# Hybrid decoder step: state-space rounds with the gelu stores issued by ScalarE, two rounds' tables loaded first, the first scan between the scaled blocks, and a table in the weight ring

## The reference, cut to what matters

```
u = h.reshape(bsz, L, S5_GROUPS, S5_GROUP)                 # 64 groups of 16 channels
bu_re, bu_im = einsum('gpc,blgc->blgp', bb, u)             # 64 complex states per group
pr, pi, sr, si = associative_scan(s5_combine, (ar, ai, bu_re, bu_im), axis=1)
y = einsum(c_re, st_re) - einsum(c_im, st_im) + d_skip * u
y = gelu(y)
pg = y @ w_glu
out = pg[..., :D] * sigmoid(pg[..., D:])
```

## Time and profile before

| what | us |
| --- | --- |
| median of 3 runs | 3763.41 |
| the profiled execution | 3765.0 |
| its span | 3763.3 |
| PE busy | 3483.8 |
| s5 phase, end of ffn0 to the first glu matmul (2571.7 to 2762.3) | 190.6 |
| PE busy in it | 99.9 |

### The profile page before, as it was taken

How to read it: one execution, slowest core, us unless ns; L and a number is a source line. 1 busy time by engine, 2 the same in 40 slices (tenths; PEclk the granted TensorE clock), 3 DMA queues, 4 the chain that set the end, 5 groups by cost and what they waited for, 6 DMA issues and landing times.

```text
span 3763.3 us, 56314 instructions
## 1 busy us (share of the span) xinstructions
PE 3483.8 (93%) x23339; PEld 3372.6 (90%) x23339; DVE 2151.3 (57%) x4475; ACT 830.3 (22%) x1753; POOL 840.4 (22%) x773
## 2 busy tenths in 40 slices
PE   6999999999999999998799999996579899999998
PEld 5989898999989898987799999995479799999997
DVE  5666768586766666775656765745622433333434
ACT  3333233323232332323001001001210200000001
POOL 2202020202020111201232322322323133333331
PEclk8999999999999999999899999998689899999999
DMA  2111111111111111110112222224821011111111
GB/s 94 47 36 47 40 42 38 53 37 47 33 50 41 47 44 44 41 34 24 36 53 82 69 77 82 64 74 145 233 55 45 28 49 49 46 45 51 46 45 63
DMA packets 106413, 214.19 MB, mean 57 GB/s; under 512 B 24240, under 2 KB 58416, under 8 KB 105136
## 3 DMA queue, kind: packets, MB, share of 16 engines
q1 hardware_dynamic: 77536, 169.20, 14.4%
q10 hardware_dynamic: 28624, 41.38, 3.4%
HBM read 169.47 MB, written 41.07 MB: 56 GB/s over the span
## 4 chain that ended last, share of the span: by engine, by line
PE 75%; DVE 19%; issue 2%; DMA 2%; ACT 1%; SPq 1%; POOL 0%; POOLq 0%; DVEq 0%; ACTq 0%
PE ps L215 23%; PE ps L585 15%; PE ps L1275 12%; PE ps L744 4%; PE ps L662 4%; PE ps L740 3%; PE ps L730 3%; PE ps L231 1%; DVE dwork L1202 1%; PE ps L637 1%; PE ps L292 1%; DVE S L1094 1%; DMA uu<-keep_u 1%; DVE n_r L1529 1%; PE ps L597 1%
## 5 line engine op out<-in xcount | busy, mean ns | idle before, releaser
L215 PE MATMUL ps<-hhi,whi 128*128 128x344 f32 x2424 | 778.8, 321 | 20.1 <-DVE hlo L1739 16.2
L215 PE MATMUL ps<-hhi,wlo 128*128 128x344 f32 x2424 | 776.1, 320 | 0.0
L215 PE MATMUL ps<-hlo,whi 128*128 128x344 f32 x2424 | 775.2, 320 | 0.0
L2004 POOL TENSOR_TENSOR wtick<-wtick 128x1 f32<-128x1 f32 x213 | 43.5, 204 | 2727.3 <-PE ps L215 828.9
L2007 POOL TENSOR_TENSOR wlo<-wraw,whi 128x1024 fp32r<-128x1024 f32 x213 | 529.9, 2488 | 17.1
L215 PEld LDWEIGHTS ps<-hhi,whi 128*128 128x128 f32 x2424 | 457.4, 189 | 22.8 <-issue 17.9
L215 PEld LDWEIGHTS ps<-hhi,wlo 128*128 128x128 f32 x2424 | 457.0, 189 | 0.0
L215 PEld LDWEIGHTS ps<-hlo,whi 128*128 128x128 f32 x2424 | 456.7, 188 | 0.1
L1364 DVE TENSOR_TENSOR ab<-ps,sg 128x344 f32<-128x344 f32 x132 | 68.2, 516 | 600.4 <-PE ps L215 583.5
L585 PE MATMUL ps<-hhi,whi 128*128 128x344 f32 x1152 | 387.1, 336 | 1.8 <-DVE dwork L952 1.8
L1275 PE MATMUL ps<-ahi,whi 128*128 128x344 f32 x1056 | 343.0, 325 | 33.5 <-DVE ab L1364 26.7
(11 more groups left out here) (345 smaller groups left out, 6226.3 us busy)
## 6 DMA issues: line engine op xcount, KB each, us to landing
wraw<-in_w SPq DMA_DIRECT2D x213, 512.0 KB, 3.5
dwork<-keep_rows SPq DMA_DIRECT2D x64, 256.0 KB, 3.2
tab<-keep_tab SPq DMA_DIRECT2D x8, 1088.0 KB, 6.5
S<-in_sin ACTq DMA_DIRECT2D x16, 512.0 KB, 3.7
out_sout<-S ACTq DMA_DIRECT2D x16, 512.0 KB, 2.7
keep_u<-hs SPq DMA_DIRECT2D x8, 580.0 KB, 3.0
uu<-keep_u SPq DMA_DIRECT2D x8, 580.0 KB, 7.8
keep_tab<-cp ACTq DMA_DIRECT2D x8, 576.0 KB, 6.5
```

Source lines behind the costliest of these rows:

```text
L215: ins = nc.tensor.matmul(out, w, r[:, kt, blk(n)], start=k == 0, stop=k == 3 * KT - 1)
```

## The change

The stores of `yg` go from SP to ACT, which issues them right after the gelu of the same round. `ee0` (scan table of the even rounds) and the inner table of the odd rounds lie in the two slots of `wraw`; the outer table of the odd rounds has its own room, and `hs` has its own; `yg` lies in the first buffer of `hs`. SP loads the tables of round 0 and the inner and outer tables of round 1 before the first block is stored; the scan table of round 1 follows the eighth block. DVE runs scan(0) after three scaled blocks and the other five after it. In SP's loop all loads of round r+2 stand before the state's store of round r, the scan table ahead of the outer one. Two fewer weight units are loaded before the phase; they follow it, behind waits for PE's inner(7) and DVE's xp(6).

```diff
-        ee0 = s_("ee0", [P, 2, PQ, NBLK])
+        ee0 = wraw[:, 1, :].rearrange("p (a q n) -> p a q n", a=2, q=PQ)
...
-        tab = [tab0, s_("tab1", [P, TABW])]
-        yg = s_("yg", [P, 2 * PQ, XC])
+        hs = s_("hs", [P, 3, STEP, UC])
+        tab1 = s_("tab1", [P, TABW - TWT])
+        inner_tab, outer_tab = [tab0[:, 0:TWT], wraw[:, 0, :]], [tab0[:, TWT:TABW], tab1[:, :]]
+        yg = hs[:, 0].rearrange("p a n -> p (a n)")[:, 0:2 * PQ * XC].rearrange("p (g n) -> p g n", n=XC)
...
-            def inputs(r):
+            def inner_table(r):
                 o = r % 2
                 if r >= 2:
                     s.after("PE", f"vv{r - 2}.1")
+                sp.dma_start(inner_tab[o], keep_tab[r, :, 0:TWT]).then_inc(inner_in[o], 16)
+
+            def load_u(r):
                 if r >= 3:
                     s.after("PE", f"y{r - 3}.1")
-                sp.dma_start(tab[o][:, 0:TWT], keep_tab[r, :, 0:TWT]).then_inc(inner_in[o], 16)
                 sp.wait_ge(u_store[r], 16)
...
-            def tables(r):
+            def outer_table(r):
+                o = r % 2
+                if r >= 2:
+                    s.after("PE", f"y{r - 2}.1")
+                sp.dma_start(outer_tab[o], keep_tab[r, :, TWT:TABW]).then_inc(outer_in[o], 16)
+
+            def scan_table(r):
                 o = r % 2
                 if r >= 2:
                     s.after("PE", f"y{r - 2}.1")
                     s.after("DVE", f"xp{r - 2}")
                     s.after("POOL", f"sto{r - 2}")
-                sp.dma_start(tab[o][:, TWT:TABW], keep_tab[r, :, TWT:TABW]).then_inc(outer_in[o], 16)
                 sp.dma_start(eel[o][:, :, :, :], keep_ee[r]).then_inc(outer_in[o], 16)
                 sp.dma_start(xp[o][:, :, :, NBLK + 1:XC], dr["s5i"][r]).then_inc(outer_in[o], 16)
...
-            tables(0)
+            inner_table(0)
+            outer_table(0)
+            sp.wait_ge(w_split, glu0 + 2)
+            inner_table(1)
+            scan_table(0)
+            outer_table(1)
             store_u(0)
-            inputs(0)
-            for kt in range(1, KT):
+            store_u(1)
+            load_u(0)
+            store_u(2)
+            load_u(1)
+            for kt in range(3, KT):
                 store_u(kt)
-            for kt in range(KT):
-                sp.wait_ge(u_store[kt], 16)
-            inputs(1)
-            tables(1)
+            scan_table(1)
             for r in range(SR):
                 if r + 2 < SR:
-                    inputs(r + 2)
-                s.after("ACT", f"ge{r}")
-                for j in range(STEP):
-                    sp.dma_start(keep_y[r].rearrange("(g c) j n -> j c g n", c=G16)[j], yg[G16 * j:G16 * (j + 1), :, :]).then_inc(y_store, 16)
-                if r + 2 < SR:
-                    tables(r + 2)
+                    inner_table(r + 2)
+                    load_u(r + 2)
+                    scan_table(r + 2)
+                    outer_table(r + 2)
...
-            for kt in range(KT):
+            def scaled(kt):
...
+            for kt in range(3):
+                scaled(kt)
             for r in range(SR):
+                if r == 1:
+                    for kt in range(3, KT):
+                        scaled(kt)
...
                         a.go(A.activation(d3, y3, AF.Gelu_apprx_tanh), f"ge{r}")
+                a.after("ACT", f"ge{r}")
+                for j in range(STEP):
+                    A.dma_start(keep_y[r].rearrange("(g c) j n -> j c g n", c=G16)[j], yg[G16 * j:G16 * (j + 1), :, :]).then_inc(y_store, 16)
...
-            weights(done, glu0 + 4)
-            s5_sync(Eng("SP", sp))
-            weights(glu0 + 4, N_UNITS)
+            weights(done, glu0 + 2)
+            E = Eng("SP", sp)
+            s5_sync(E)
+            E.after("PE", f"vv{SR - 1}.1")
+            E.after("DVE", f"xp{SR - 2}")
+            weights(glu0 + 2, N_UNITS)
```

More of the change, by code:

```diff
@@ L1437, in build @@
         tab0 = s_("tab0", [P, TABW])
-        hsc = ctx.enter_context(ExitStack())
-        hs = sb("hs", [P, 3, STEP, UC], F32, hsc)
-        hsc.close()
-        tab = [tab0, s_("tab1", [P, TABW])]
-        yg = s_("yg", [P, 2 * PQ, XC])
+        hs = s_("hs", [P, 3, STEP, UC])
+        tab1 = s_("tab1", [P, TABW - TWT])
+        inner_tab, outer_tab = [tab0[:, 0:TWT], wraw[:, 0, :]], [tab0[:, TWT:TABW], tab1[:, :]]
+        yg = hs[:, 0].rearrange("p a n -> p (a n)")[:, 0:2 * PQ * XC].rearrange("p (g n) -> p g n", n=XC)
         s5c.close()
-        wtl = [t_[:, 0:TWT].rearrange("p (a q n) -> p a q n", a=2, q=PQ) for t_ in tab]
-        cpl = [t_[:, TWT:TWT + TCP].rearrange("p (a q k c) -> p a q k c", a=2, q=PQ, c=G16) for t_ in tab]
-        htl = [t_[:, TCP + TWT:TABW].rearrange("p (g n) -> p g n", n=P) for t_ in tab]
+        wtl = [t_.rearrange("p (a q n) -> p a q n", a=2, q=PQ) for t_ in inner_tab]
+        cpl = [t_[:, 0:TCP].rearrange("p (a q k c) -> p a q k c", a=2, q=PQ, c=G16) for t_ in outer_tab]
+        htl = [t_[:, TCP:TABW - TWT].rearrange("p (g n) -> p g n", n=P) for t_ in outer_tab]
         eel = [ee0, tmp]
@@ L1648, in inputs @@
                     s.after("PE", f"vv{r - 2}.1")
+                sp.dma_start(inner_tab[o], keep_tab[r, :, 0:TWT]).then_inc(inner_in[o], 16)
+            def load_u(r):
                 if r >= 3:
                     s.after("PE", f"y{r - 3}.1")
-                sp.dma_start(tab[o][:, 0:TWT], keep_tab[r, :, 0:TWT]).then_inc(inner_in[o], 16)
                 sp.wait_ge(u_store[r], 16)
-                sp.dma_start(uu[r % 3][:, :, :], keep_u[r].rearrange("(g c) j n -> (c j) g n", c=G16)).then_inc(inner_in[o], 16)
-            def tables(r):
+                sp.dma_start(uu[r % 3][:, :, :], keep_u[r].rearrange("(g c) j n -> (c j) g n", c=G16)).then_inc(inner_in[r % 2], 16)
+            def outer_table(r):
[4 more added lines that the diff above has]
+            def scan_table(r):
                 o = r % 2
```

## The result

The changed kernel is slower. Its median is 3786.12 us (3779.47 to 3788.74, 5 runs) against 3763.41 (3760.28 to 3767.21, 5 runs); the ratio is 1.0057, with an interval of 1.0043 to 1.0072, so 16 to 27 us.

What follows compares the result with a forecast made beforehand. The table loop (34.45 us for two rounds) was taken to bound the kernel, with ACT's copy of vv just under it. Gelu(7) 13.1 us later plus 0.2 of tail made +13.3, so 3777 us against the median; range 3762 to 3789.

Steps and rivals of the forecast that it cites:

- The mechanism: In the rounds, ACT's issues delay high, low, smp and the copy to vv, which then comes last, 14.6 us after gelu.
- Rival A: In the rounds, only the table loop counts; a pair drops by 5.0 to 29.5 us, time 3753.5; chance 0.08.
- the 3.1 us of spare: In the kernel before, ACT's copy of vv ends 3.1 us ahead of the tables, so it costs nothing there.
- B: Rival: PE runs at 2.4 GHz in the loop, a pair takes 30.2 us, not slower at 3763.7; chance 0.13.
- D: Rival: tables late for another reason, loop stays 34.45, only the late round 1 remains: +7.5, 3771; chance 0.05.
- C: Rival: low wholly on each scan and stalled ACT issues, 4.3 us a pair: 3790, the first alone 3782; chance 0.14.
- Gelu(1) at 2656.9: Start of the phase: round 1's late scan table makes gelu(1) end 7.5 us later than before; bounds 2651.3 and 2660.0.
- PE has idled before, so 10.7: In round 1, outer(1) with its gelu takes 10.7 us at 1.2 GHz, not 6.55 at 2.4 GHz.
- The pair of 34.5: Gelu to gelu over two rounds: 33.6 us plus 0.9 for the low; three pairs to gelu(7) take 103.5.
- 0.9, as the overlap is partial: POOL's low beside DVE's rotations costs 0.9 us a pair, bounds 0 and 2.6; the upper adds about 5 us overall.
- The tail, +0.2: After gelu(7), ACT's issues take 3.86 us in place of 3.67; the weight units that follow cost 0.
- The sum: Whole kernel: 13.1 to gelu(7) plus 0.2 of tail, +13.3 us; 3778.3 profiled, 3777 against the median.

Runs made afterwards that it cites:

- e1: The kernel before, with only the eight stores of yg moved to ACT behind the gelu: 3778.73 us, ratio 1.0028 to before.
- e2: The changed kernel with the stores back on SP, behind the loads of round r+2: 3769.38 us, ratio 1.0000 to before.
- e3: The changed kernel with high(r-1) on ACT between gelu(r) and the eight issues: 3768.60 us, ratio 1.0007 to before.
- e9: The changed kernel with POOL's sample step of round r+1 ahead of low(r-1): 3764.18 us, ratio 1.0001 to before.
- e6: The changed kernel with four of the eight stores issued by ACT and four by SP behind the loads: 3771.12 us, ratio 1.0011 to before.
- e8: The changed kernel with all eight blocks ahead of scan(0) and the stores on SP behind the loads: 3759.30 us, ratio 0.9978 to before.
- e7: The changed kernel with all eight scaled blocks ahead of scan(0), stores still on ACT: 3768.17 us, ratio 1.0003 to before.

## Why the prediction came out as it did

**The mechanism was right.** It said that the copy to vv takes the place of the tables as the last wait ahead of L1760 (L1775 now), and that a high starts 4 us behind its gelu: in rounds 3, 5 and 7 32.3 us of waiting for vv against 0.3 for tables in the whole phase, and 4.6 us. Gelu(7) ended at 2764.1 on before's scale, for 2760.4. e1 shows that the issues alone bring the loss, e2 that it goes with them, e3 and e9 that it is gone, as far as can be told, when either the high or smp comes out from behind its neighbour, e6 that half the issues give half.

**Rival A** (only the table loop counts, 3753.5) fell: e2 and e8 take the tables off the path without the issues on ACT, and gain 0.0 and 8.3 us. The other loops lie close enough under it, as the 3.1 us of spare showed. **B** (2.4 GHz) fell: outer(3), (5) and (7) ran at 1.29 us for eight matmuls, half speed, after gaps of PE of 5.0, 5.3 and 17.8 us; outer(4) and (6) ran at full speed, but their gelus stand behind the copy on ACT and came no earlier for it. **D** (tables late for another reason) fell with the 0.3 us. **C**, more on the path, is where the kernel moved: 3786 lies between its 3782 and 3790, and both its parts came: the low at its full price, and issues that SP's loads slow, by less than it had.

**Gelu(1) at 2656.9.** Too late by 4.8: it ended at 2653.0, or 2652.1 on before's scale. The scans began about where they should (2609.1 and 2635.2 on before's scale, for 2610.3 and 2636.0), gelu(0) ended at 2635.9 for 2636.4. The failed step is "PE has idled before, so 10.7": inner(2) ended 1.8 us ahead of outer(1), whose eight matmuls took 0.74 us, full speed, and outer with gelu took 6.5, the other bound of that sentence. Of the 7.5 us, 2.7 came.

**The pair of 34.5.** It took 37.34; three of them make 8.5 us, the largest part of what is missing. Term by term, from gelu(1)'s end at 2653.01 to gelu(3)'s at 2690.36:

| term | predicted | measured |
|---|---|---|
| issues | 3.86 | 4.6 (2653.04 to the high at 2657.62) |
| high to the end of the copy | 9.42 | 9.4 (2657.62 to 2667.00) |
| scan with the low on it, hand-offs | 10.1 + 0.9 + 0.25 | 12.7 (2667.00 to 2679.68) |
| outer and gelu | 10.0 | 10.7 (2679.68 to 2690.36) |
| sum | 34.5 | 37.35 |

The mis-sized term is the low on the scan, 1.6 us: not "0.9, as the overlap is partial" but the upper bound, 2.5 (3.22 for 0.69). Of a low that began inside the scan's 10 us no part was free: the three rotations began 0.85, 1.28 and 1.53 us after their low and each lost 2.53 us. Only a low that was under way before the scan started cost less (in e9 the first operation of three scans took 2.10 us, with the low 1.3 us old). The Trainium skill (SBUF — State Buffer, "Who interferes with whom") says that a VectorE instruction with two SBUF inputs contends with a GpSimd instruction that reads SBUF, and that what they share is an exclusive lock. The 3.22 us agree with it, and so do the lows that grew; the sum that the prediction gave by that rule was nearer. Next the issues, 0.7: the rate came from a stretch in which SP issued one weight unit beside ACT's sixteen issues, but here SP issues round r+2's loads at the same moment (L1668 at 2689.48 and ACT's first store at 2690.39); the last eight, with no load of tables beside them (2765.05), took 3.70. Last outer and gelu, 0.7: cold throughout, the upper bound again.

**The tail, +0.2.** It was +2.2: the step "after gelu(7) ACT's issues take 3.86 in place of 3.67" counted the issues and not what was queued behind them, the very fault that it found in the loop. The last load of yl is issued at 2774.13, right behind the end of low(6) at 2774.07; low(6) waits for high(6), which begins 3.78 us after the gelu. e1 has it too (17.0), and e2, with the stores on SP, doesn't (13.9).

**The sum.** Predicted +7.5, +5.6, +0.2 (13.3); measured +2.7, +14.1, +2.2 (19.0). Two errors of opposite sign hid part of each other; the total was 5.7 off in the profiled execution and 9 in the medians. That the time came out inside the range is in part luck: the three pairs grew by 14.1 us where 5.6 were forecast.

**What stays open.** Why the stores on ACT cost about 10 us with the blocks first and about 20 with scan(0) between them; how much of it is PE's clock and how much the chain itself. The parity on which the low falls fits e7's pair, but the order of the blocks doesn't set it alone, as e1 has the blocks first and the low on odd scans. And e1's profiled execution (+17) and its ratio (+10.5) differ, so within one kernel the phase isn't the same in each run; its other runs have no trace.

## What to carry to other kernels

Before an instruction or a set of DMA issues is moved to another engine, follow what is queued behind it there to its consumers on the third and fourth engine: here 4 us of issues stood ahead of a high, a low, a sample, a copy, a scan and a gelu, in a loop with 3.1 us to spare. If a stop behind it can be put out of the way (the high ahead of the issues, the sample ahead of the low), the same issues are free. When a wait for a DMA is 34 us in sum, what it is worth is the distance to the next loop under it, not the 34. Look also at what a later consumer does to PE: of the 4.7 us that a pair lost here, 2.5 stand in outers with their gelus, which ran at 1.2 GHz where it had been 2.4. And where a contention blocks whole instructions, take the upper of its two bounds.

## What the runs showed of the hardware that was not expected

- POOL's low (128x1024, a difference of two SBUF tiles) stopped one DVE operation for as long as the low still had to run, whether it was a rotation or a scan: a 128x512 rotation took 3.22 to 3.37 us in place of 0.69, the group of eight scans 5.23 to 5.27 in place of 2.62. In the kernel after the low itself grew from 2.86 to 3.52, 3.95 and 4.20 us, by 0.2 us less than it had begun ahead of the stopped rotation (0.85, 1.28 and 1.53).
- Eight DMA issues on ACT took 3.70 us with no loads of tables beside them, and 3.8 to 5.6 beside those of SP (4.77 at 2690.39; 5.62 in e3), that is 0.46 us each and up to 0.70. SP's own issue of an outer table took between 0.66 and 2.67 us in the rounds of the kernel after (2652.86 and 2636.17).
- Of PE's clock: after a gap of 5.0 us PE ran the whole of outer(3) at 1.2 GHz (1.29 us for eight matmuls from 2679.68 on, 9.8 us at work); after a gap of 1.8 us it ran the whole of outer(1) at 2.4 GHz (0.74 us, from 2646.48 on). Ahead of either gap stood an inner that had run at 1.2 GHz (4.13 us for its 32 matmuls, at 2670.53 and 2640.56; 2.20 at 2.4 GHz, at 2689.38).
